# Moving weight loads of layer 0 forward: pairs 1 and 2 of the experts, output weights by column halves, second router weights in their own place

## The reference

```
layer 0: x += concat(gated_mlp(norm(x)), sparse_attention(norm(x))) @ w_out
         x += moe(norm(x), layer 0)
layer 1: x += (pooled(norm(x)) @ w_pool + b_pool) * pool_scale
         x += moe(norm(x), layer 1)

moe: logits of 4 groups and of 32 experts (8 in each group); top-1 group, top-2 experts in it
     y = sum over the two chosen experts of  p_e * (silu(x @ w_gate[e]) * (x @ w_up[e])) @ w_down[e]
```

## Time and profile before

| what | us |
|---|---|
| median of 3 runs | 896.33 (894.91 to 896.59) |
| the profiled execution, its own time | 892.19 |
| its span (first to last instruction) | 890.4 |
| PE busy | 791.5 (89% of the span) |
| 16 DMA engines busy, queue of SP | 69.2% of the span |
| HBM read | 247.44 MB |

### The profile page before, as it was taken

The page is one execution under the profiler, slowest core; times in us unless marked ns, Lnnn a source line. Parts: engine busy times, 40 slices in busy tenths (PEclk is TensorE's granted clock), DMA queues, the critical chain, the costliest instruction groups (busy, mean ns, idle before and its releaser), DMA issues.

```text
span 890.4 us, 10328 instructions
## 1 busy us (share of the span) xinstructions
PE 791.5 (89%) x3981; PEld 375.3 (42%) x3981; DVE 255.4 (29%) x577; ACT 242.6 (27%) x584; POOL 100.1 (11%) x164
## 2 busy tenths in 40 slices
PE   6999899999999989998877978899999996797965
PEld 3447444555555633333322322397433332332321
DVE  0100727566462351111101111554511111111106
ACT  3303355554344411221101111364012211111111
POOL 2000000000002510111101001130111111011000
PEclk9999999999999999999988999999999999888998
DMA  8898130200002599999999999996399999999986
GB/s 287 259 328 189 64 78 18 95 2 1 0 1 79 205 404 406 416 357 421 421 421 419 419 415 391 386 421 252 141 392 418 419 419 423 420 420 418 406 312 253
DMA packets 74912, 258.09 MB, mean 290 GB/s; under 512 B 28017, under 2 KB 29553, under 8 KB 54896
## 3 DMA queue, kind: packets, MB, share of 16 engines
q1 hardware_dynamic: 65936, 241.16, 69.2%
q0 software_dynamic: 8928, 16.27, 4.9%
HBM read 247.44 MB, written 26.21 MB: 307 GB/s over the span
## 4 chain that ended last, share of the span: by engine, by line
PE 71%; DMA 10%; DVE 8%; issue 4%; ACT 3%; SPq 3%; DVEq 1%; POOLq 0%
PE ps L1884 22%; PE ps L1898 10%; PE ps L1611 10%; PE ps L1762 6%; DMA rest<-in_w_exp_down_dram 5%; PE ps L1878 3%; PE ps L1674 3%; PE ps L1818 2%; PE ps L1573 2%; PE ps L1686 2%; PE ps L1830 2%; SPq L442 2%; DMA norm<-expert_rows 2%; PE ps L2013 2%; PE ps L1591 2%
## 5 line engine op out<-in xcount | busy, mean ns | idle before, releaser
L1884 PE MATMUL ps<-w_pair,tmp 128*64 128x512 f32 x704 | 172.1, 644 | 38.1 <-issue 17.7
L1884 PEld LDWEIGHTS ps<-w_pair,tmp 128*64 128x64 f32 x704 | 55.8, 148 | 140.2 <-issue 124.9
L1611 PE MATMUL ps<-w_pair,norm 128*128 128x512 f32 (+1 forms) x256 | 100.5, 552 | 4.2 <-DMA w_pair<-in_w_in_dram 3.7
L1077 DVE TENSOR_TENSOR tmp<-tmp,ps 128x256 f32<-128x256 f32 (+1 forms) x34 | 13.8, 407 | 294.7 <-ACT tmp L962 294.7
L962 ACT ACTIVATE tmp<-ps 128x256 f32<-128x256 f32 x32 | 12.3, 384 | 272.4 <-PE ps L1884 272.4
L1898 PE MATMUL ps<-w_pair,tmp 128*64 128x512 f32 x352 | 80.4, 598 | 3.2 <-ACT tmp L965 2.0
L1884 PE MATMUL ps<-norm,tmp 128*64 128x512 f32 x320 | 72.8, 607 | 10.5 <-issue 7.3
L1611 PEld LDWEIGHTS ps<-w_pair,norm 128*128 128x128 f32 x256 | 48.8, 193 | 52.3 <-issue 45.2
L657 POOL DMA_INDIRECT expert_rows<-tmp x30 | 30.2, 1005 | 331.1 <-DVE tmp L1467 314.2
L1762 PE MATMUL ps<-w_pair,norm 128*128 128x512 f32 x128 | 58.0, 593 | 0.0
L957 ACT ACTIVATE tmp<-ps,gains 128x128 f32<-128x128 f32 x128 | 36.6, 369 | 61.1 <-PE ps L1878 61.1
(11 more groups left out here) (241 smaller groups left out, 832.7 us busy)
## 6 DMA issues: line engine op xcount, KB each, us to landing
w_pair<-in_w_exp_gate_dram SPq DMA_DIRECT2D x44, 1024.0 KB, 17.6
w_pair<-in_w_exp_up_dram SPq DMA_DIRECT2D x44, 1024.0 KB, 26.1
w_pair<-in_w_exp_down_dram SPq DMA_DIRECT2D x40, 1024.0 KB, 26.9
rest<-in_w_exp_down_dram SPq DMA_DIRECT2D x20, 1024.0 KB, 22.1
norm<-in_w_exp_gate_dram SPq DMA_DIRECT2D x20, 1024.0 KB, 23.1
norm<-in_w_exp_up_dram SPq DMA_DIRECT2D x20, 1024.0 KB, 27.6
norm<-expert_rows SPq DMA_DIRECT2D x16, 512.0 KB, 8.3
w_pair<-in_w_in_dram SPq DMA_DIRECT2D x3, 2048.0 KB, 10.1
```

The costliest lines, as they stand in the source:

```text
L1611: ins = mm(bank(4 + i % 4)[:, 0:n], xT[:, k, b * P:(b + 1) * P], w[:, k, :], start=(k == 0), stop=(k == KD - 1))
L1884: ins = mm(bank(2)[64 * a:64 * a + 64, :], xgT[:, k, 64 * a:64 * a + 64], gu[w][:, a, :, k * FE:(k + 1) * FE], start=(k == 0), stop=(k == ...
```

## The change

1. `wout` is kept as two column halves. Half 1 (columns 512 to 1023) lies in columns 4096 to 8191 of `w_pair1`, half 0 in columns 0 to 4095. `load_wout(1)` is issued where the first part of the weights was, `load_wout(0)` where the second was. Each has three DMAs, with rows of 2 KB instead of 4 KB. `out_proj` waits for the half that it reads.
2. `pool_sc` moves from `rest` to columns 4864 to 5887 of `tmp`. The routing table's work area lies there too, so VectorE (DVE) gets a wait on `s_pbs` in `route`, before it builds `OA`.
3. The router weights of layer 1 get a place of their own, in two pieces in `tmp` and `mix_small`. They are loaded (four DMAs in place of two, the same elements) when attention is over, and POOL multiplies them with the gain before `experts(0)`. The router weights of layer 0 are loaded and multiplied in two pieces too.
4. `load_down(0, 1)` and `load_down(0, 2)` are issued when attention is over. `load_gate_up(0, 1, 0)` waits for the first half of the last block's output projection alone and stands behind the store of rows 0; `load_gate_up(0, 1, 1)` waits for the second half and stands behind the store of rows 3. The wait of SP for POOL's scaling is gone.

```
@@ -135,7 +135,7 @@
-        wout = W1[:, 0:8192].rearrange("p (k n) -> p k n", k=KD)
+        wout = [W1[:, 4096 * h:4096 * h + 4096].rearrange("p (k n) -> p k n", k=KD) for h in range(2)]
@@ -174,7 +174,7 @@
-        pool_sc = R[:, 0:1024]
+        pool_sc = TMP[:, 4864:5888]
@@ -387,13 +386,17 @@
+        w_route = [[w.rearrange("p (k c) -> p k c", k=4) for w in pieces]
+                   for pieces in ((w_r[:, 0:144], w_r[:, 144:288]), (TMP[:, 5984:6128], mix[:, 512:656]))]
...
+            for h in range(2):
+                ks = slice(4 * h, 4 * h + 4)
+                eng.dma_start(w_route[l][h][:, :, 0:4], rg[:, ks, :]).then_inc(s_wr, 16)
+                eng.dma_start(w_route[l][h][:, :, 4:36], rexp[:, ks, :]).then_inc(s_wr, 16)
@@ -496,12 +499,18 @@
+            def load_wout(h):
+                c = slice(512 * h, 512 * h + 512)
+                for g in range(2):
+                    rows = t["w_out"][0, 512 + 256 * g:768 + 256 * g, c]
+                    sp.dma_start(wout[h][HD * g:HD * g + HD, 4:8, :], rows.rearrange("(i d) n -> d i n", d=HD))\
+                      .then_inc(s_wout[h], 16)
+                sp.dma_start(wout[h][:, 0:4, :], t["w_out"][0, 0:512, c].rearrange("(k p) n -> p k n", p=P))\
+                  .then_inc(s_wout[h], 16)
+
+            load_wout(1)
             sp.wait_ge(s_pj, 20)
+            load_wout(0)
@@ -512,18 +521,18 @@
                     sp.dma_start(pool_sc, t["pool_scale"].to_broadcast([P, D])).then_inc(s_poolw, 16)
+                    load_down(0, 1)
+                    load_down(0, 2)
+                    load_router(sp, 1)
                 for b in range(NB):
-                    if l == 0 and b == NB - 1:
-                        sp.wait_ge(s_ps, 2)
-                        sp.wait_ge(s_pbs, 1)
-                        load_down(0, 2)
-                        sp.wait_ge(s_op, 2 * NB)
-                        load_gate_up(0, 1, 0)
                     sp.wait_ge(s_xs[b], n)
                     sp.dma_start(norm_dram[b * P:(b + 1) * P, :], xs[:, b, :]).then_inc(s_st, 16)
+                    if l == 0 and b == 0:
+                        sp.wait_ge(s_op, 2 * NB - 1)
+                        load_gate_up(0, 1, 0)
                 if l == 0:
+                    sp.wait_ge(s_op, 2 * NB)
                     load_gate_up(0, 1, 1)
-                    load_down(0, 1)
@@ -539,8 +548,6 @@
-                    if l == 0 and i == 5:
-                        load_router(sp, 1)
@@ -664,8 +671,6 @@
-                    if l == 0 and i == 8:
-                        gain_router(1)
@@ -736,6 +742,7 @@
+            gain_router(1)
             pool.wait_ge(s_zst, 16)
             experts(0)
@@ -1405,6 +1412,7 @@
+                dve.wait_ge(s_pbs, 1)
@@ -1749,7 +1756,7 @@
-                    pe_.wait_ge(s_woutb, 32)
+                    pe_.wait_ge(s_wout[half], 48)
```

More of the change, by code:

```diff
@@ L207, in build @@
         s_ws = sem("ws_loaded")
-        s_wout = sem("wout_first_half_loaded")
-        s_woutb = sem("wout_second_half_loaded")
+        s_wout = sems("wout_loaded", 2)
         s_poolw = sem("pool_weights_loaded")
@@ L388, in build @@
         assert at[0] <= 3840, at[0]
+        w_route = [[w.rearrange("p (k c) -> p k c", k=4) for w in pieces]
+                   for pieces in ((w_r[:, 0:144], w_r[:, 144:288]), (TMP[:, 5984:6128], mix[:, 512:656]))]
         def load_router(eng, l):
[L392 to L396, removed]
+            rg = t["w_router_group"][l].rearrange("(p k) g -> p k g", k=KD)
+            rexp = t["w_router_expert"][l].rearrange("(p k) g e -> p k (g e)", k=KD)
+            for h in range(2):
+                ks = slice(4 * h, 4 * h + 4)
+                eng.dma_start(w_route[l][h][:, :, 0:4], rg[:, ks, :]).then_inc(s_wr, 16)
+                eng.dma_start(w_route[l][h][:, :, 4:36], rexp[:, ks, :]).then_inc(s_wr, 16)
         block = ctx.enter_context(nc.Block())
@@ L498, in _ @@
             sp.wait_ge(s_pj, 16)
[L499 to L502, removed]
+            def load_wout(h):
[7 more added lines that the diff above has]
+            load_wout(1)
             sp.wait_ge(s_pj, 20)
-            sp.dma_start(wout[:, 0:4, :], t["w_out"][0, 0:512, :].rearrange("(k p) n -> p k n", p=P)).then_inc(s_wout, 16)
+            load_wout(0)
             for l in range(LAYERS):
@@ L706, in gain_router @@
             def gain_router(l):
[L707 to L710, removed]
+                pool.wait_ge(s_wr, 64 * (l + 1))
+                for h in range(2):
+                    wr = w_route[l][h]
+                    g.tensor_tensor(wr, wr, gain_v[:, 1 + 2 * l, 4 * h:4 * h + 4].unsqueeze(2).to_broadcast([P, 4, 36]),
+                                    ALU.mult).then_inc(s_wrg, 1)
             gain_router(0)
@@ L1585, in logits @@
             def logits(l, b):
-                wr = w_r[:, :].rearrange("p (k c) -> p k c", k=KD)
-                pe_.wait_ge(s_wrg, l + 1)
+                pe_.wait_ge(s_wrg, 2 * (l + 1))
                 pe_.wait_ge(s_rxa, NB * l + b + 1)
@@ L1590, in logits @@
                 for k in range(KD):
-                    ins = mm(bank(LOGIT_BANK[l])[:, b * 36:(b + 1) * 36], rx[b % 2][:, k, :], wr[:, k, :],
+                    ins = mm(bank(LOGIT_BANK[l])[:, b * 36:(b + 1) * 36], rx[b % 2][:, k, :], w_route[l][k // 4][:, k % 4, :],
                              start=(k == 0), stop=(k == KD - 1))
@@ L1759, in out_proj @@
                     if k == 0:
-                        pe_.wait_ge(s_wout, 16)
                         pe_.wait_ge(s_yv, 2)
-                    ins = mm(out_bank(b, half), xT[:, k, b * P:(b + 1) * P], wout[:, k, half * 512:(half + 1) * 512],
+                    ins = mm(out_bank(b, half), xT[:, k, b * P:(b + 1) * P], wout[half][:, k, :],
                              start=(j == 0), stop=(j == KD - 1))
```

## The result

| | us |
|---|---|
| before, median of 11 runs | 896.33 (891.49 to 897.16) |
| after, median of 11 runs | 889.84 (888.02 to 893.94) |
| ratio after / before | 0.9938, 95% interval 0.9921 to 0.9956 |
| predicted | 895.7, range 893.3 to 897.2 |
| profiled execution after, own time (span) | 889.84 (888.1) |

By the ratio the change saves 5.6 us (by its interval 3.9 to 7.1); the two medians stand 6.5 apart, and the executions of the kernel before spread over 5.7. I had forecast 0.6 and no measurable change. The result lies on the side of rival A, and beyond the price that I gave it (2.2 to 3.7 us).

What follows compares the result with a forecast made beforehand. The full DMA stream of expert weights was taken to set layer 0's end. The emptied queue and removed router loss gave 0.4 us, PE's start 0.2, other parts 0: 0.6 off 896.33 makes 895.7, range 893.3 to 897.2.

Steps and rivals of the forecast that it cites:

- rival A: Layer 0's experts: the lead is kept to the end and a shorter stream ends earlier; 892.6 to 894.1, chance 0.27.
- The DMA stream sets the end of the experts: End of layer 0: set by the last weights of the full stream, at 418 GB/s, 15.0 us per pair.
- The head start becomes idle time: Before pair 3's first load: pair 2's gates land at 333, not 342.0, and the stream idles until PE frees the slot.
- SP was free of the small pieces: SP's queue after attention: the router's issues hold it 18.8 us from 287, to about 306.
- Layer 1 as the model of an emptied queue: Layer 1's experts, loaded ahead, show what reaches layer 0's end without backlog and router loss: 0.4 us.
- my bound of 3.3 from the window 380 to 400: Layer 0's stream at the router load: the whole rate loss, 348 against 418 GB/s, the most that can reach the end.
- Pair 9: Middle of layer 0's experts: begins about 2 us earlier after the change, at 449.8, as layer 1 was 2.0 ahead.
- PE's start, 0.2: PE's first pair in layer 0: a faster gather starts it 0.2 us earlier, between 0 and 0.4.
- The other parts, 0: Output weights by halves, DVE's wait on `s_pbs`, POOL's gain in two halves, matmul sizes: each hidden or unchanged, 0 us.
- B: Layer 0's first gather: stores land too late and each us counts whole; slower, 899.7 to 906, chance 0.10.
- a first gather after 323: Start of layer 0's experts: a first gather starting after 323 would show the stores came too late.
- moving them saves only if the new place has slack: Router's small pieces: they cost the same anywhere, so moving pays only with slack; by the sum, just enough after attention.

Runs made afterwards that it cites:

- router_late: Changed kernel with layer 1's router weights loaded and multiplied at their old times (pairs 5 and 8); 896.39 us, ratio to before 0.9997.
- router_only: Kernel before with only the early load of layer 1's router weights, right after attention, into places of their own; 893.31 us, ratio to before 0.9964.
- before_packed: Kernel before with layer 1's router weights still loaded at pair 5, but as 384 whole rows in 3 DMAs; 893.05 us, ratio to before 0.9966.
- before_warm: Kernel before with 50 filling matmuls in place of 46 ahead of layer 0's pair 0; 897.2 us, ratio to before 1.002.
- before_again2: Kernel before, unchanged, profiled once more after before_again; 896.73 us, one execution.
- before_again: Kernel before, unchanged, in a second profile; 898.12 us, one execution.
- downs_late: Changed kernel with the down weights of pairs 1 and 2 loaded at their old places; 892.99 us, ratio to before 0.9971.
- packed_fill30: Changed kernel, layer 1's router weights in whole rows at pair 5, 30 filling matmuls in place of 46 ahead of layer 0's pair 0; 889.61 us, one execution.
- packed_fill30b: Same kernel as packed_fill30, unchanged, in a second profile; 891.31 us, one execution.
- gates_late: Changed kernel with pair 1's first gates waiting for the whole output projection, ahead of the store of rows 3; 891.8 us, ratio to before 0.995.
- last_down_whole: Changed kernel with pair 15's down weights in 2 DMAs with 8 KB rows instead of 4 with 2 KB, both layers; 893.13 us, ratio to before 0.9946.
- packed_late: Changed kernel with layer 1's router weights loaded at pair 5 in whole rows (3 DMAs); 888.73 us, ratio to before 0.9905.

## Why the prediction was wrong

- **The DMA stream sets the end of the experts: right in the main.** The load that I read at the end of the chain was pair 14's, not the last of the stream, and a second way to the end runs through pair 15's weights. After the change the chain of layer 0 ends in PE in one profile, 0.8 us behind pair 14's landing, and in pair 15's weights in the other.
- **The head start becomes idle time: right.** Last gates of pair 2 predicted to land at 333, landed at 333.5 at the latest; all stores landed by 317.36, when pair 2's gates go out (predicted 317 to 319). SP was free of the small pieces at 299.5, not 305 to 306. The share from 316 to 336 is 0.80; in router_late 0.64 and no gain that can be seen.
- **The failed step: "Layer 1 as the model of an emptied queue".** I took the difference between layers, 0.4 us, for what would reach the end. What reached it is the whole loss of the router's pieces: my bound of 3.3 from the window 380 to 400, against 3.2 us in the chain, 3.2 in router_only and 3.0 in before_packed (both by the ratio). I had the number and threw it away for a comparison of layers. Layer 1 was the wrong twin: its stage is 229.0 to 229.4 in nearly all profiles, of before and after alike, while layer 0 without the pieces reaches 226.6 to 227.3. Pair 14's down weights go out at 827.26 - 637.30 = 190.0 after PE's start in layer 1, in layer 0 now at 187.3, and in layer 1 SP is held 9.21 us in the issue just before them (`818.01`). Why layer 1 loses this in its tail isn't shown. Pair 9 was also off: 451.31 - 333.84 = 117.5 against 118.7 before, 1.2 earlier and not 2.0. The model erred in the middle in one direction and at the end in the other.
- **PE's start, 0.2: about right.** After attention's end PE starts 50.02 and 50.16 in two profiles after, 50.46, 50.57 and 50.69 in three of before: 0.5.
- **The other parts, 0: not contradicted**, they were not tried one by one. Attention ended at 282.4 to 285.6 in all kernels, with no order between before and after.
- **Missing: the clock.** The sum had no term for PE's first pair. Before the change the gather leaves PE a gap of 0.4 to 0.6 us, after it 0.1 to 0.4, and with whole rows on top of it none. A fall costs 1.7 us, and 1 of 3 profiles of before had it, 0 of 2 after. That the average of the runs gains by it isn't shown; before_warm, which closed the gap, was slower.
- **What stays open:** stage 3.3 (mean of 229.46, 230.81 and 229.99 against that of 226.94 and 226.62) and start 0.5 make 3.8, about the lower end of the measured 3.9 to 7.1. By the first sums it is 3.3 for the stage as well (236.00 against 232.70). The other 1.8 of 5.6 is not placed. The profiles of before have falls of the clock elsewhere that those of after lack, in parts that the change leaves alone: granted clock 0.57 from 583 to 591 in before_again2, where the pooling mixer takes 3 us longer, and a last gate_up of 5.25 in layer 1 of before_again, 1.3 us later at its first sum. Five profiles can't tell whether such falls are rarer after the change or came by chance. The gap between router_only and after is 2.3 us by the ratios, and their intervals overlap; downs_late suggests that some of it is the down weights' early place, through the gather.
- **The rivals:** A was the right side, and its condition (an earlier end of a full stream) the right mechanism. B did not come. Its sign, a first gather after 323, is met by 0.14 (323.14, 0.8 later than before), but attention had ended 1.15 later too, at 283.83, and the stores were no part of it: pair 2's gates, which wait for them, went out 4.8 us before the routing table was ready (322.17). The Trainium skill's rule in "DMA: Bandwidth & Descriptors", section "Why small descriptors are slow", is in line with before_packed: fewer, larger rows at the same place brought the 3 us (it changed SP's hold too). With my reading "moving them saves only if the new place has slack" the runs agree: at attention's end the engines had idle time anyway (share 0.23 from 292 to 304).

## What to carry to other kernels

When the trace shows a loss of rate in a stream that ends a stage, price the edit by that loss (bytes missing divided by the stream's rate; here 3.3 against 3.0 to 3.3 measured), and treat a comparison with a similar stage as a weaker witness, unless the similar stage has been seen to reach the same end. Find every way that leads to the end of a stage, not only the one that the chain of one execution took: here the reload and the last pair took turns. Before moving a load made of small pieces, try to load it in whole rows and reorder it on an idle engine. Filling matmuls ahead of a wait are to last just until it ends: more of them stand on the path, and with fewer PE's clock may fall over the phase behind (packed_fill30 and its repeat: 1.6 and 2.4 us won at its start and 1.7 lost in it).

## What the runs showed of the hardware

- In the full stream the DMA of the router's small pieces held SP's queue 13.76 us and the next issue 5.01 (before); at attention's end the last of four such DMAs held it 9.24 (after). The same weights as 384 whole rows took 0.43 per issue (before_packed). Large loads are held in the full stream too: 13.08 us for one of pair 14's gate and up loads in before (498.98).
- PE idle for 1.2 to 1.7 us, then 1.2 us once more behind 8 transposes, went with a granted clock of one half over 3.4 us of the next phase, 7.09 to 8.78 or 8.48, in 3 of 3 profiles (packed_fill30, packed_fill30b, downs_late); with 0.65 in one of one (gates_late); with 0.1 to 0.6 us in 3 of 8.
- The second of pair 14's two loads of 1 MB, issued into a stream of 414 to 418 GB/s, landed 21.4 to 21.9 us after its issue in both layers, before and after. In layer 1 of last_down_whole it took 24.5 and landed at the same time after PE's start, as it was issued earlier.
- The first gather took 8.26 us with pair 2's weights still in the queue (after) and 5.2 with the queue emptied sooner (packed_late).
